# 32 more bytes of padding in front of the activations' tiles of a two-block float32 model

## The reference

```python
def peer_ffn(x, w_q, sub_keys, exp_u, exp_v):
    q = (x @ w_q).reshape(B, T, PEER_HEADS, 2, PEER_DKEY // 2)
    s = jnp.einsum('bthcd,hcnd->bthcn', q, sub_keys)
    ...   # the 16 best of 256 pairs of keys, per token and head; their softmax is the gate
    def block(args):
        xb, ib, gb = args
        h = jax.nn.gelu(jnp.einsum('md,mkd->mk', xb, exp_u[ib]), approximate=False)
        coef = (gb * h).astype(xb.dtype)
        return jnp.einsum('mk,mkd->md', coef, exp_v[ib])
```

## Time and profile before

| | |
|---|---|
| median of 3 runs | 2762.49 us (2757.74 to 2766.14) |
| the profiled execution: its own time, its span | 2759.51 us, 2757.7 us |
| TensorE (PE) busy | 2488.6 us, 90% |
| weight loads (PEld) | 2354.4 us, 85% |
| VectorE (DVE) busy | 1829.6 us, 66% |
| ScalarE (ACT) busy | 1356.6 us, 49% |
| GpSimd (POOL) busy | 635.5 us, 23% |

### The profile page before, as it was taken

One profiled execution on the slowest core, in us unless ns is written; L12 is line 12 of the kernel. 1 busy time (PEld: TensorE's weight loads), 2 busy tenths in 40 slices (PEclk: granted clock), 3 DMA queues, 4 the chain that ended last, 5 costly groups with the idle time before them and its releaser, 6 DMA issues. The chain is left out here.

```text
span 2757.7 us, 61487 instructions
## 1 busy us (share of the span) xinstructions
PE 2488.6 (90%) x22160; PEld 2354.4 (85%) x22160; DVE 1829.6 (66%) x4121; ACT 1356.6 (49%) x2453; POOL 635.5 (23%) x490
## 2 busy tenths in 40 slices
PE   5899686878895899999999999878989999999997
PEld 3699466467895899999999999767989999999997
DVE  6622723447644497688899766584895887999665
ACT  6631534345312555555544555444656555444554
POOL 0246034127403595000000000334890000000000
PEclk9999898999997999999999999889999999999999
DMA  9722012124201344444444445313445444444452
GB/s 299 236 86 88 1 58 84 46 66 135 77 2 54 117 171 175 174 162 157 161 160 167 168 183 186 119 62 104 165 154 188 162 167 158 163 155 164 183 185 89
DMA packets 153714, 374.29 MB, mean 136 GB/s; under 512 B 8640, under 2 KB 102736, under 8 KB 136944
## 3 DMA queue, kind: packets, MB, share of 16 engines
q1 hardware_dynamic: 151072, 369.73, 38.7%
q10 hardware_dynamic: 2512, 2.82, 0.3%
HBM read 371.48 MB, written 1.05 MB: 135 GB/s over the span
## 5 line engine op out<-in xcount | busy, mean ns | idle before, releaser
L2525 ACT ACTIVATE w_hi<-ring 128x512 fp32r<-128x512 f32 x1024 | 643.6, 632 | 715.4 <-PE bank L2580 367.5
L2531 DVE TENSOR_TENSOR w_lo<-ring,w_hi 128x512 fp32r<-128x512 f32 x864 | 593.8, 690 | 317.7 <-ACT w_hi L2525 303.9
L2562 PE MATMUL bank<-x_hi,w_hi 128*128 128x256 f32 x2048 | 586.0, 286 | 22.8 <-POOL w_lo L2531 20.3
L2580 PE MATMUL bank<-hidden_hi,w_hi 128*128 128x256 f32 x2048 | 583.5, 285 | 0.6 <-ACT hidden_hi L2650 0.6
L2562 PE MATMUL bank<-x_lo,w_hi 128*128 128x256 f32 x2048 | 572.0, 279 | 0.0
L2580 PE MATMUL bank<-hidden_lo,w_hi 128*128 128x256 f32 x2048 | 571.6, 279 | 0.0
L2580 PE MATMUL bank<-hidden_hi,w_lo 128*128 128x256 f32 x2048 | 571.2, 279 | 0.0
L2562 PE MATMUL bank<-x_hi,w_lo 128*128 128x256 f32 x2048 | 570.7, 279 | 0.0
L359 POOL TENSOR_TENSOR w_lo<-ring,w_hi 128x512 fp32r<-128x512 f32 (+2 forms) x264 | 348.6, 1337 | 752.2 <-ACT w_hi L350 743.4
L2562 PEld LDWEIGHTS bank<-x_hi,w_hi 128*128 128x128 f32 x2048 | 385.2, 188 | 27.0 <-ACT w_hi L2525 18.4
L2580 PEld LDWEIGHTS bank<-hidden_hi,w_hi 128*128 128x128 f32 x2048 | 385.4, 188 | 0.8 <-ACT hidden_hi L2650 0.8
(11 more groups left out here) (510 smaller groups left out, 4417.7 us busy)
## 6 DMA issues: line engine op xcount, KB each, us to landing
ring<-in_peer_uT SPq DMA_DIRECT2D x128, 1024.0 KB, 4.8
ring<-in_peer_v SPq DMA_DIRECT2D x128, 1024.0 KB, 4.7
ring<-in_even_w_in SPq DMA_DIRECT2D x26, 1024.0 KB, 5.1
ring<-in_ada_w SPq DMA_DIRECT2D x24, 1024.0 KB, 7.2
ring<-in_odd_w_in SPq DMA_DIRECT2D x12, 1024.0 KB, 5.2
ring<-in_even_w_out SPq DMA_DIRECT2D x8, 1024.0 KB, 4.8
ring<-in_odd_w_out SPq DMA_DIRECT2D x8, 1024.0 KB, 5.1
ring<-in_peer_w_q SPq DMA_DIRECT2D x8, 1024.0 KB, 5.3
```

The source lines that it names most:

```text
L2525: act.activation(k.hi[q][:, :], k.ring[slot][:, q * PART:q * PART + PART], ACT.Copy).then_inc(k.hi_ready, 1)
L2531: eng.tensor_tensor(k.lo[q][:, :], k.ring[slot][:, q * PART:q * PART + PART], k.hi[q][:, :].bitcast(F32), ALU.subtract).then_inc(k.lo_read ...
L2562: mm = pe.matmul(k.bank[s][:, j * T:j * T + T], a[q][:, w], b[:, cc, :], start=(cc == 0 and n == 0), stop=(cc == KC - 1 and n == 2))
L2580: mm = pe.matmul(out, a[q][:, w], b[:, j, :], start=first and cc % 2 == 0 and n == 0, stop=last and cc % 2 == 1 and n == 2, skip_group_che ...
```

## The change

`before_x` is 64 bytes per partition instead of 32. Nothing uses it. The instructions of every engine, their order and their waits are the same, row for row (7549 rows of the program for TensorE, 1760 for VectorE, 941 for ScalarE, 179 for GpSimd, 156 for SyncE). What differs is the place of each tile behind the padding: all lie 32 bytes higher.

```diff
@@ -3021,7 +3021,7 @@
         k = Core(nc, ctx, d)
         plan_weights(k)
 
-        k.sb("before_x", [P, 8])
+        k.sb("before_x", [P, 16])
         k.xh, k.xl = k.sb("x_hi", [P, KC, T], F32R), k.sb("x_lo", [P, KC, T], F32R)
         with k.room():
             setup(k)
```

## The result

The changed kernel takes 2771.2 us (median of 8 runs, 2768.2 to 2774.9), the kernel before, measured beside it, 2762.8 (8 runs, 2757.7 to 2766.1). The ratio is 1.0033, with a 95% interval of 1.0023 to 1.0044: slower by 8.4 us. I had forecast slower by 22.0. The profiled execution took 2770.2 us with a span of 2768.4, 10.7 more than the span before; what follows is worked out in the spans.

What follows compares the result with a forecast made beforehand. TensorE's matmul pace was taken as the bound. Terms of +22.3, -0.6, +0.6, +1.3 and -1.6 made +22.0 us on the profiled 2759.5, so 2781.5; plus 3.0 for the median, 2784.5 us, range 2756 to 2815.

Steps and rivals of the forecast that it cites:

- What bounds the kernel: Long feed-forward stretches: only the pace of TensorE's matmuls sets the time; TensorE busy 90% of the span.
- No cost elsewhere: ScalarE, VectorE and transfers: nothing to gain or lose that would show; VectorE has 17% of each long stretch free.
- The price on TensorE: Feed-forward and projection matmuls: gap goes from 116.67 to 118.33 ns, 13,440 matmuls by 1.66 ns, +22.3 us.
- The base: Starting gap of 116.67 ns, read in the down phase, taken for all 13,440 matmuls.
- The gates: 3,072 gate matmuls of 30 ns, both operands moving: 1.4% more each, +1.3 us.
- The cover: First part of the up phase: slower matmuls fill TensorE's waits for GpSimd, half of 3.2 us, -1.6 us.
- The projections: 1,536 projection matmuls: most slow by 1.66 ns within the +22.3 us; 384 of `xn1` and `mixT1` gain, -0.6 us.
- The rule weighed against the trace: TensorE: the skill's independent read ports would make the sum 0; its 109 ns estimate was set against the traced 116.67.
- No change: Rival: TensorE's pace stays at 116.67 ns, a floor many placements reach; 2762 us, within 3; chance 0.28.
- Slower, 120: Rival: TensorE gap 120 ns or beyond, both reads on the same half of 64 bytes; 2811 us; chance 0.20.
- Faster, 113.3: Rival: TensorE's lost 10 ns end when both reads begin alike; 113.3 ns, -46 us, 2716; chance 0.12.
- The prediction's own last sentence: Wrong if the TensorE gap follows distance to the weight parts or the stretch's starting phase, not the moving operand's remainder.

Runs made afterwards that it cites:

- the grid: Both blocks left out of the kernel; only 72 sections of 96 matmuls, at varied operand distances and entries; mean gaps about 113.3 to 120.0 ns, no kernel time given.
- s64_m96: Against the kernel before: 32 bytes added ahead of the weight parts, activations where the changed kernel has them, operand distance 32; 2759.9 us, ratio 1.0000.
- g13_d32: The kernel before with one more gate matmul at the head of each group, 13 instead of 12; 2771.6 us, ratio 1.0045.
- p0: The kernel before with the padding before x_hi left out; 2790.5 us, ratio 1.0110 against before.
- p160: The kernel before with the padding before x_hi made 160 bytes; 2780.1 us, ratio 1.0063 against before.
- g13_d192: The kernel before with 192 bytes of padding and 13 gate matmuls a group instead of 12; 2746.4 us, ratio 0.9955 against before.
- p192: The kernel before with the padding before x_hi made 192 bytes; 2766.7 us, ratio 1.0015 against before.

## Why the prediction was right in direction and wrong in size

- **What bounds the kernel: right.** Counts of instructions, waits, VectorE, ScalarE and the clock are the same; the 10.7 us of the span are TensorE's pace, 10.9 of them in the feed-forward layers.
- **No cost elsewhere: right.** VectorE +1.3 us busy, ScalarE -0.5, both hidden.
- **The price on TensorE: the step that failed.** "I take 118.33, the row with the moving remainder that all get." The gap became 117.78. The rows chosen as nearest have the weight part moving, so their distances are counted the other way round: 32 less 128 for `xn`, which is 160 modulo 256, and 32 less 64 for `x`, which is 224. The feed-forward after the change has 64. They were near in remainder, and far in what counts: the grid gives 118.6 or 117.3 at 160, 118.4 at 224, and 117.8 at 64 with 13 or 17 small ones ahead (113.3 with 12). The variable itself was wrong, as s64_m96 shows: the moving remainder of the change with no change in time. The direction came out right with a wrong variable, and that is luck: *d* = 64 has a pace below 116.67 too, and by the grid's numbers the same padding would have made the kernel faster with all stretches in that one.
- **The base: also off.** 116.67 was read in a pure down phase and taken for all 13,440. The feed-forward average before was higher, 116.67 throughout only in the two down phases. Together: 12,288 by 1.66 is 20.4 us forecast, 12,288 by 0.89 is 10.9 measured. That is 9.5 of the 11.3 us that the forecast was too long in the span.
- **Small terms.** The gates: +1.3 forecast, 0.0 measured (134.1 us both times). The cover: -1.6 forecast, nothing seen, since TensorE's idle time in the first up stretch is 11.6 us in both kernels. The projections: their 1,152 others at +1.66 would be +1.9; all that lies outside the feed-forward phases came to -0.2, because some distances got better (`mixT1` from 96 to 128, 120.0 to 118.67; `mixT2` from 160 to 192, 117.33 to 113.33) and some didn't (`xn1` stays at 120.0, the first token projection went from 118.67 to 120.0). The tail's +1.5 I didn't trace; it takes 22.1 us in before and 25.1 in g13_d32, both at *d* = 32, so distance alone doesn't set it.
- **The rule weighed against the trace.** The Trainium skill (TensorE: Matmul & The Clock Gate, Step-by-step: what each phase is for) has two independent read ports, and I had read from it that the meeting of the two reads is free. For bf16 the grid agrees: no distance changes anything. The same page's Back-to-back issue gap section gives N/2.4 + 2.5 for an isolated matmul at the full clock, an estimate of 109.2 ns for 256 columns. The grid's bf16 measured 109.16. For the fast float32 format the runs disagree with both, 113.3 to 120.0. With 4 stationary columns 113.34 is left at most distances: so 4.2 ns of the surplus over bf16 come without a full weight load, and up to 6.7 more with one.
- **The rivals.** "No change" is not what happened, and 116.67 is no floor that many placements reach: with 128 stationary columns it was seen at *d* = 32 only. "Slower, 120" exists: at *d* = 0 and 96 throughout, at 128 and 160 in places. "Faster, 113.3" exists too, at *d* = 192: I had named as its mechanism that both reads begin alike, and that is shown false, since p0 has just that and runs at 120.0; in the changed kernel both begin alike modulo 64, and it runs at 117.8. The prediction's own last sentence named the true variable, the distance to the weight parts, as what would make it wrong, but gave it no number. The rows at hand had paces for some distances (`x` at 32 116.67, `xn1` and `mixT1` at 96 120.0, `xn` at 160 118.67), but none for 64, to which the change went.

**What stays open.** What in the entry chooses between the paces: the number of small matmuls ahead matters, but not it alone. Distance 224 wasn't tried in the feed-forward layers; the token projections with `x` stationary had it before, at 118.3. At *d* = 128 the changed kernel has 118.67 in some projections and 120.0 in others (`xn1`, the first token projection), while the grid has 118.6 to 118.8 only; the grid also lacks the 120.0 that p160 has at *d* = 160. bf16 and 4 columns were tried with one entry only. That the two reads hinder each other is an inference, from the distance that decides and from the 4 columns that take most of the effect away; no run shows where they would.

## What to carry to other kernels

In this stream of fast float32 matmuls of 256 columns, which keeps TensorE busy, the distance modulo 256 bytes between the starts of the stationary and the moving operand was worth 1.3% of the kernel's time between the best and the worst padding alone (2760.9 and 2799.1 us), and costs only bytes. Of the distances tried, 0 and 96 were the slowest, at 119.7 to 120.0 ns in every phase. 32 kept between 116.7 and 117.8. 192 reached 113.3 in some stretches and 117.8 in others, depending on how they were entered. Move one tile against the other and look at *pairs*, never at one tile's remainder. Read the pace from two beginnings 60 matmuls apart, in each stretch by itself, since the mean ns of a group (286 before and after here, for the first form of the up phase) doesn't show it.

## What the hardware did that I hadn't expected

- The paces are few: 113.33, 116.67, 117.33, 117.78, 118.67 and 120.0 ns are found in the grid and in the full kernel alike (the grid's 118.38 at *d* = 224 is a seventh, near the 118.3 of the token projections before). A stretch without a pause stays in one of them: both down phases of the changed kernel average 117.78 over 1536 matmuls each.
- Two of them are open to the same operands at the same places, in one kernel (before: 7.00 us for 60 at 1020 us and 7.06 at 1090 us; g13_d192: 6.80 and 7.07 in its two down phases).
- One more matmul ahead of each group of gates made the kernel 20 us faster (2766.7 for p192, 2746.4 for g13_d192; measured beside different runs of before, 2762.6 and 2759.9).
